# Final RMS norm: applying the scale per token as the transposed rows leave PSUM

## The reference

```python
def rmsnorm(x, g):
    xf = x.astype(jnp.float32)
    y = xf * lax.rsqrt(jnp.mean(xf * xf, axis=-1, keepdims=True) + RMS_EPS)
    return (y * g.astype(jnp.float32)).astype(x.dtype)

def trunk(x, S_init, make_ctx, attend):
    for l in range(DEPTH):
        ...
        x = x + o
        x = x + sq_relu_mlp(rmsnorm(x, norm_mlp[l]), w_mlp_up[l], w_mlp_down[l])
    return rmsnorm(x, norm_final), jnp.stack(new_S), new_kv
```

## Time and profile before

| | us |
|---|---|
| median of 3 runs | 2034.08 (2032.62 to 2037.61) |
| the profiled execution | 2034.55 |
| its span, first to last instruction | 2032.9 |
| TensorE busy (matmul) | 1908.7 (94%) |
| VectorE, ScalarE, GpSimd busy | 896.5 (44%), 489.1 (24%), 417.0 (21%) |

### The profile page before, as it was taken

One profiled execution on the slowest core, in us unless ns is written; L12 is line 12 of the kernel. 1 busy time (PEld: TensorE's weight loads), 2 busy tenths in 40 slices (PEclk: granted clock), 3 DMA queues, 4 the chain that ended last, 5 costly groups with the idle time before them and its releaser, 6 DMA issues.

```text
span 2032.9 us, 27497 instructions
## 1 busy us (share of the span) xinstructions
PE 1908.7 (94%) x10540; PEld 1588.8 (78%) x10540; DVE 896.5 (44%) x1296; ACT 489.1 (24%) x1007; POOL 417.0 (21%) x613
## 2 busy tenths in 40 slices
PE   6999999898999999999989989799867899999997
PEld 6888888677888888888856668687535788888886
DVE  3555555515453535310157763244520355353544
ACT  3344434321101010200235543233310211111101
POOL 2232433210000000200036653342020100000002
PEclk9999999899999999999979999899988999999998
DMA  5232221112222222223850008896997022222221
GB/s 146 72 87 64 65 75 64 64 42 83 83 83 83 83 83 84 94 72 95 221 126 1 1 1 173 207 190 159 300 303 245 1 83 83 83 83 83 83 83 43
DMA packets 164708, 207.22 MB, mean 102 GB/s; under 512 B 13905, under 2 KB 101570, under 8 KB 164450
## 3 DMA queue, kind: packets, MB, share of 16 engines
q1 hardware_dynamic: 146818, 186.84, 31.9%
q10 hardware_dynamic: 16416, 14.95, 2.3%
q0 software_dynamic: 1344, 3.67, 0.5%
HBM read 194.33 MB, written 18.42 MB: 105 GB/s over the span
## 4 chain that ended last, share of the span: by engine, by line
PE 85%; DVE 3%; ACTq 2%; DMA 2%; SPq 2%; issue 2%; ACT 2%; POOL 1%; DVEq 0%; POOLq 0%
PE ps L1209 39%; PE ps L1000 12%; PE ps L1039 11%; PE ps L1300 5%; PE ps L1293 3%; PE ps L1079 2%; DMA stream<-in_cache_nsa_kv 2%; PE ps L1054 2%; PE ps L1349 1%; ACTq L2007 1%; PE ps L1371 1%; PE ps L1389 1%; ACTq L428 1%; PE ps L1145 1%; PE ps L1105 1%
## 5 line engine op out<-in xcount | busy, mean ns | idle before, releaser
L1039 PE MATMUL ps<-h,stream 128*128 128x260 f32 x1024 | 236.3, 385 | 5.1 <-DVE h L2129 5.1
L1209 PE MATMUL ps<-big,scratch 128*128 128x260 f32 x1024 | 232.3, 382 | 0.0
L1039 PEld LDWEIGHTS ps<-h,stream 128*128 128x128 f32 x1024 | 191.3, 191 | 37.0 <-issue 10.0
L1209 PEld LDWEIGHTS ps<-big,scratch 128*128 128x128 f32 x1024 | 194.6, 190 | 29.9
L2276 DVE TENSOR_TENSOR scratch<-stream 128x1024 f32<-128x1024 f32 x64 | 106.1, 1699 | 223.6 <-PE ps L1209 214.8
L796 POOL TENSOR_TENSOR big<-big 128x520 f32<-128x520 f32 x32 | 51.7, 1616 | 713.5 <-ACT big L1820 713.5
L1209 PE MATMUL ps<-big,stream 128*128 128x260 f32 x768 | 176.2, 382 | 0.0
L1209 PEld LDWEIGHTS ps<-big,stream 128*128 128x128 f32 x768 | 145.9, 190 | 22.4
L1000 PE MATMUL ps<-h,stream 128*128 128x260 f32 x640 | 142.4, 386 | 1.7 <-DVE h L2705 1.7
L1000 PEld LDWEIGHTS ps<-h,stream 128*128 128x128 f32 x640 | 122.7, 192 | 21.1 <-DVE h L2705 1.9
L1209 PE MATMUL ps<-h,stream 128*128 128x260 f32 x512 | 120.2, 389 | 9.1 <-DVE h L2299 9.1
(11 more groups left out here) (363 smaller groups left out, 3016.6 us busy)
## 6 DMA issues: line engine op xcount, KB each, us to landing
stream<-in_w_mlp_up SPq DMA_DIRECT2D x16, 2048.0 KB, 8.1
stream<-in_w_mlp_down SPq DMA_DIRECT2D x16, 2048.0 KB, 7.9
stream<-in_cache_nsa_kv SPq DMA_DIRECT2D x128, 256.0 KB, 6.1
stream<-in_w_hgrn_in SPq DMA_DIRECT2D x32, 512.0 KB, 6.9
stream<-in_cache_nsa_kv SPq DMA_DIRECT2D x114, 128.0 KB
stream<-in_cache_nsa_kv ACTq DMA_DIRECT2D x114, 128.0 KB
stream<-in_cache_win_kv SPq DMA_DIRECT2D x16, 512.0 KB
out<-in_cache_win_kv SPq DMA_DIRECT2D x8, 1022.0 KB
```

The lines of the kernel that those rows point to most:

```text
L1039: m = nc.tensor.matmul(pair(c)[:, a, :], w[:, k, :], h[:, k, NH * a:NH * a + NH], start=(k == 0), stop=(k == KD - 1))
L1209: m = nc.tensor.matmul(ps[:, BANK[r] + q, 0:NH], w[:, k, q, :], operand(p, r)[:, k, :], start=(r not in (2, 3, 4) and k == 0), stop=(k == ...
```

## The change

The norm's gain and its per-token scale are taken apart.

The gain moves to ScalarE, as the first layer does it: `mlp_act(1, GAIN_FINAL)` writes `h = x * gain` as each piece of `x` becomes final. The transposes then turn `h` without the token's scale, so they need not wait for the norm: groups 0 and 1 come ahead of the sum of squares (they use banks 6 and 7), groups 2 and 3 right behind it, 4 to 7 after those.

The sum of squares is made with the roles swapped: the squares are the stationary operand and one column of ones the moving one, so token `i` of a tile comes out on partition `i`. There are five tiles (four of 128 tokens, one of 8), and `rstd` is 128 by 5 in place of 128 by 520. Tiles 0 and 1 need only GpSimd's sum; tiles 2 to 4 also take rows 4 and 6. Tile 2 holds tokens 256 to 259 of the first half, for which rows 4 and 6 are in the sum already, so GpSimd sets those columns to zero first.

The copies out of PSUM become multiplications by the token's scale, a number for each partition: `tensor_scalar` on VectorE, `activation` with a scale on ScalarE.

```diff
+        Y_BANK = (6, 7, 0, 1, 2, 3, 6, 7)
...
-        out_count = {..., "final": 6 * KD + 4}
+        out_count = {..., "final": 6 * KD + 8}
...                                                        # GpSimd, mlp_pool
                 joined(last)
+                if name == "final":
+                    ch.link(nc.gpsimd.memset(squares[:, 4:8:2, 2 * P:NH], 0.0))
                 piece_added(3, 1, 1)
...                                                        # TensorE
-            norm_sum("final", squares)
+            def rows_turned(u):
+                a, cg = u % TT, u // TT
+                if u >= 6:
+                    pe.wait_ge(ydone[u % 2], 1)
+                for c in range(4):
+                    m = nc.tensor.transpose(ps[:, Y_BANK[u], P * c:P * c + P], h[:, 4 * cg + c, P * a:P * a + P], ident[:])
+                m.then_inc(yturned, 1)
+
+            until(pe, "u2", 2 * PAIRS)
+            pe.wait_ge(norm["out"], out_count["mlp1"] + 4)
+            rows_turned(0)
+            rows_turned(1)
+            pe.wait_ge(norm["added"], turn_of["final"])
+            until(pe, "c", 2 * PAIRS)
+            for a in range(TT + 1):
+                cols = slice(P * a, min(P * a + P, N))
+                rows = (0,) if a < 2 else (0, 4, 6)
+                if a == 2:
+                    pe.wait_ge(norm["sq"], steps_before(SQ_STEPS, "final") + 5)
+                for k in rows:
+                    m = nc.tensor.matmul(ps[0:cols.stop - cols.start, 5, a:a + 1], squares[:, k, cols], ones[:, 0:1],
+                                         start=(k == 0), stop=(k == rows[-1]))
+            m.then_inc(norm["sum"], 1)
+            until(pe, "dve_a", kind_count(2 * PAIRS, "down"))
+            rows_turned(2)
+            rows_turned(3)
             until(pe, "d", 2 * PAIRS)
-            until(pe, "dve_a", kind_count(2 * PAIRS, "down"))
-            for u in range(2 * TT):
-                a, cg = u % TT, u // TT
-                if a == 0:
-                    pe.wait_ge(norm["out"], out_count["final"] - KD // 2 * (1 - cg))
-                if u >= 4:
-                    pe.wait_ge(ydone[u % 2], (u - 4) // 2 + 1)
-                for c in range(4):
-                    m = nc.tensor.transpose(ps[:, u % 4, ...], h[:, 4 * cg + c, ...], ident[:])
-                m.then_inc(yturned, 1)
+            pe.wait_ge(norm["out"], out_count["final"])
+            for u in range(4, 2 * TT):
+                rows_turned(u)
+            for p in range(2):
+                pe.wait_ge(ydone[p], 2)
             for c in range(KD):
-                m = nc.tensor.transpose(ps[0:B, 4 + c // 4, ...
+                m = nc.tensor.transpose(ps[0:B, c // 4, ...
...                                                        # ScalarE
-            mlp_act(1)
-            root("final")
+            mlp_act(1, GAIN_FINAL)
+            act.wait_ge(norm["sum"], turn_of["final"] + 1)
+            nc.scalar.activation(rstd[:, 0:TT], ps[:, 5, 0:TT], ACT.Sqrt, bias=eps[:], scale=1.0 / D).then_inc(norm["sqrt"], 1)
+            nc.scalar.activation(rstd[0:B, TT:TT + 1], ps[0:B, 5, TT:TT + 1], ACT.Sqrt, bias=eps[0:B], scale=1.0 / D)\
+                .then_inc(norm["sqrt"], 1)
+            act.wait_ge(token_rstd, 1)
             for u in range(1, 2 * TT, 2):
                 act.wait_ge(yturned, u + 1)
-                nc.scalar.activation(yrows[...], ps[:, u % 4, :], ACT.Copy).then_inc(ydone[1], 1)
+                nc.scalar.activation(yrows[...], ps[:, Y_BANK[u], :], ACT.Copy,
+                                     scale=rstd[:, u % TT:u % TT + 1]).then_inc(ydone[1], 1)
...                                                        # VectorE
-            norm_dve("final")
-            for k in range(KD):
-                nc.vector.scalar_tensor_tensor(out=h[:, k, :], in0=x[:, k, :], scalar=vec[...], in1=rstd[:], ...)
+            n = steps_before(SQRT_STEPS, "final")
+            dve.wait_ge(norm["sqrt"], n + 2)
+            nc.vector.reciprocal(rstd[:, 0:TT], rstd[:, 0:TT]).then_inc(token_rstd, 1)
+            nc.vector.reciprocal(rstd[0:B, TT:TT + 1], rstd[0:B, TT:TT + 1]).then_inc(token_rstd, 1)
+            dve.wait_ge(token_rstd, 2)
             for u in range(0, 2 * TT, 2):
                 dve.wait_ge(yturned, u + 1)
-                nc.vector.tensor_copy(yrows[...], ps[:, u % 4, :]).then_inc(ydone[0], 1)
+                nc.vector.tensor_scalar(yrows[...], ps[:, Y_BANK[u], :], rstd[:, u % TT:u % TT + 1], None, ALU.mult)\
+                    .then_inc(ydone[0], 1)
```

More of the change, by code:

```diff
@@ L269, in steps_before @@
             return sum(steps[other] for other in steps if turn_of[other] < turn_of[name])
-        out_count = {"mix0": KD, "mlp0": 2 * KD, "kv": 3 * KD + 4, "attn": 4 * KD + 4, "mlp1": 5 * KD + 4, "final": 6 * KD + 4}
+        out_count = {"mix0": KD, "mlp0": 2 * KD, "kv": 3 * KD + 4, "attn": 4 * KD + 4, "mlp1": 5 * KD + 4, "final": 6 * KD + 8}
         squares = scratch[:, 0:KD * N].rearrange("p (k t) -> p k t", k=KD)
@@ L381, in hybrid_step @@
         block = ctx.enter_context(nc.Block())
-        hready = sem("hready")
+        hready, token_rstd = sem("hready"), sem("token_rstd")
         ydone, ysdone = [sem("ydone0"), sem("ydone1")], sem("ysdone")
@@ L970, in norm_sum @@
                 n = turn_of[name]
-                if name in ("attn", "final"):
+                if name == "attn":
                     pe.wait_ge(norm["added"], n)
@@ L1636, in _ @@
+            m.then_inc(norm["sum"], 1)
+            until(pe, "dve_a", kind_count(2 * PAIRS, "down"))
+            rows_turned(2)
+            rows_turned(3)
+            until(pe, "d", 2 * PAIRS)
+            pe.wait_ge(norm["out"], out_count["final"])
[3 more added lines that the diff above has]
+                pe.wait_ge(ydone[p], 2)
             for c in range(KD):
-                m = nc.tensor.transpose(ps[0:B, 4 + c // 4, P * (c % 4):P * (c % 4) + P], h[:, c, T:N], ident[:])
+                m = nc.tensor.transpose(ps[0:B, c // 4, P * (c % 4):P * (c % 4) + P], h[:, c, T:N], ident[:])
@@ L2084, in _ @@
             norm_act("mlp1", squares, added("nsa_out"), early=[(GAIN_MLP + KD, gained_h)])
-            mlp_act(1)
-            root("final")
+            mlp_act(1, GAIN_FINAL)
[4 more added lines that the diff above has]
+            act.wait_ge(token_rstd, 1)
             for u in range(1, 2 * TT, 2):
                 act.wait_ge(yturned, u + 1)
-                nc.scalar.activation(yrows[:, u % TT, 512 * (u // TT):512 * (u // TT) + 512], ps[:, u % 4, :], ACT.Copy)\
-                    .then_inc(ydone[1], 1)
+                nc.scalar.activation(yrows[:, u % TT, 512 * (u // TT):512 * (u // TT) + 512], ps[:, Y_BANK[u], :], ACT.Copy,
+                                     scale=rstd[:, u % TT:u % TT + 1]).then_inc(ydone[1], 1)
         @block.vector
@@ L2710, in _ @@
             mlp_pairs(1)
-            norm_dve("final")
-            for k in range(KD):
-                nc.vector.scalar_tensor_tensor(out=h[:, k, :], in0=x[:, k, :],
-                                               scalar=vec[:, GAIN_FINAL + k:GAIN_FINAL + k + 1], in1=rstd[:],
-                                               op0=ALU.mult, op1=ALU.mult).then_inc(norm["out"], 1)
+            n = steps_before(SQRT_STEPS, "final")
[3 more added lines that the diff above has]
+            dve.wait_ge(token_rstd, 2)
             for u in range(0, 2 * TT, 2):
                 dve.wait_ge(yturned, u + 1)
-                nc.vector.tensor_copy(yrows[:, u % TT, 512 * (u // TT):512 * (u // TT) + 512], ps[:, u % 4, :])\
-                    .then_inc(ydone[0], 1)
+                nc.vector.tensor_scalar(yrows[:, u % TT, 512 * (u // TT):512 * (u // TT) + 512], ps[:, Y_BANK[u], :],
+                                        rstd[:, u % TT:u % TT + 1], None, ALU.mult).then_inc(ydone[0], 1)
             dve.wait_ge(yturned, 2 * TT + 1)
-            nc.vector.tensor_copy(ysrows.rearrange("p (c n) -> p c n", c=2), ps[0:B, 4:6, :]).then_inc(ysdone, 1)
+            nc.vector.tensor_scalar(ysrows.rearrange("p (c n) -> p c n", c=2), ps[0:B, 0:2, :], rstd[0:B, TT:TT + 1], None,
+                                    ALU.mult).then_inc(ysdone, 1)
 _INS = ["x_prompt", "x_sample", "cache_nsa_kv", "cache_win_kv", "state_hgrn", "page_table", "norm_mix", "norm_mlp",
```

1 line of the change is left out of this document (removed).

## The result

| | before | changed |
|---|---|---|
| median of 14 runs, us | 2036.82 (2032.03 to 2040.82) | 2028.32 (2023.76 to 2031.97) |
| ratio to before, 95% interval | | 0.9956 (0.9947 to 0.9966) |
| profiled execution: own time, span | 2034.55, 2032.9 | 2023.76, 2022.1 |

The changed kernel is faster by 8.5 us, 0.44%.

The account below looks back on a forecast made before the run. The end was taken to stand 7.74 us behind the first store's issue; replacing 11.46 us from sum to issue by 2.12, less 0.80 for the dearer sum, saves 8.54: from median 2034.08 to 2025.5, range 2023.3 to 2028.3.

Parts of the forecast that it names:

- gain rows, memset: ScalarE's gain rows beside the last pair's products and GpSimd's 0.10 us memset of a few columns: costed at nothing.
- transposes ahead and two sums done: Eight transposes (0.8 us) and two sums (0.43) in TensorE's hole before the last square ends, done at about 2012.2.
- sum of squares ends: Nine one-column matmuls behind the last square end at 2014.50, 0.80 us later than before (bounds 0.5 to 1.0).
- first store issued: SyncE's first 1 MB store, set by the copies of groups 0 to 3, moves from 2025.16 to 2016.62.
- tail shortened by: First store's issue falls 8.54 us earlier and the end follows, to 2024.36.
- The central step: The stores, not the transposes, set the end, which stands 7.74 us behind the first issue.
- Root, reciprocal and hand-overs: Between sum and copies, two narrow roots and two reciprocals with hand-overs: 0.7 us taken, bounds 0.5 to 1.2.
- the copies: VectorE copies groups 0 and 2 in 1.28 us; ScalarE takes 0.60 plain or 0.72 scaled each; these set the first store.
- The step on the clock: TensorE keeps full clock in the new tail, since 0.50 showed only behind a 7 us idle stretch; transposes take 0.10 us.
- Rival 1: Clock falls to 0.50 from the first wait at about 2012; 5.4 us gained, 2028.7; chance 0.08.
- Rival 2: Stores run slower beside busy copying engines and TensorE, 300 GB/s: 1.5 us lost, 2027.0; chance 0.10.
- Rival 3: TensorE runs out of instructions in the tail; a stall decides from 8.5 us up, 13.3 gives 2038.8; chance 0.03.

Follow-up runs that it names:

- e5: Kernel before with the gain alone moved to ScalarE, wide root and reciprocal kept, VectorE multiplying eight rows by the scale; tail 20.90 us (21.05 before).
- e3: Changed kernel with the first 1 MB store held back until all eight groups are copied, so both go together; tail 15.00 us (12.33 in the changed kernel).
- e10: Kernel of e2 with nine useless transposes filling TensorE's pause between the sum and the scale; tail 16.74 us.
- e2: Changed kernel with all groups turned only when the per-token scale is ready; tail 15.23 us, first store at 7.42.
- e11: Kernel of e2 run once more, unchanged; tail 14.87 us, first store at 7.04.
- e4: Kernel before with 64 useless transposes in TensorE's idle stretch between the sum and the first rows; tail 20.50 us (21.05 before).
- e1: Changed kernel with groups 0 and 1 turned right behind the sum of squares instead of ahead of it; tail 12.88 us (12.33 in the changed kernel).
- e7: Kernel of e6 with the two 1 MB stores cut into four of 512 KB, each issued when its pair is copied; tail 11.34 us, ratio to before 0.9960.
- e6: Changed kernel with row 0's sum matmuls of all five tiles and group 1's transposes ahead of the last square, sums in another bank; tail 11.95 us.
- e8: Kernel of e7 with the sums' bank cleared by its first matmul alone and group 1 turned behind the sum; tail 11.22 us, ratio to before 0.9953.
- e9: Kernel of e3 run once more, unchanged; tail 13.72 us, first issue at 5.98.

## Why the prediction was right

Its steps, measured from the last square's start (2011.85 in the prediction's times):

| step | predicted | measured |
|---|---|---|
| gain rows, memset | hidden | hidden: 21.02 us for the last pair (again in e5: 21.01) |
| transposes ahead and two sums done | 0.35 | 0.52, still ahead of the square's end |
| sum of squares ends | 2.65 | 2.42 |
| VectorE's first scaled copy | 3.38 | 3.13 |
| first store issued | 4.77 | 4.57 |
| from there to the end | 7.74 | 7.76 |
| tail shortened by | 8.54 | 8.72 |

The central step, that the end follows the first store and not the transposes, was confirmed in each of the 14 profiled executions: the end stood 7.74 to 7.84 us behind the first issue, with that issue anywhere from 3.4 to 13.3 us behind the square. The spread of 0.1 is that of the printed span.

The term that was mis-sized is the sum of squares. The prediction has 1.28 us for the six matmuls with full weights, 0.54 for the three with 8-column weights and 0.14 for the last one's end. The stretches of the changed kernel show the six and then the three (columns as in the earlier trace rows):

```profile
2010.46:2011.88 1.42, 1.42 (x12) 1.41 (x12) 0.00 (x0) 0.76 (x2) 0.00 (x0) 1.00 0.04 12
2011.88:2012.12 0.24, 0.24 (x8) 0.20 (x7) 0.00 (x0) 0.00 (x0) 0.00 (x0) 1.00 0.00 0
```

The six took 1.42 us (0.24 each, not 0.21) and the three 0.24 (0.08 each, not 0.18), and 0.07 passed to the sum's end. Two errors of opposite sign, 0.14 too little and 0.30 too much, partly cancelled; what was left is the 0.2 us by which all later steps came early. Where it did no harm: the two sums ahead waited for x21, which was added only 0.1 us before the square began, and so ended at 0.52 and not at 0.35, while the square released the rest at 0.69.

Root, reciprocal and hand-overs (0.73 predicted from the sum's end to VectorE's copy, 0.71 measured) and the copies (1.39 predicted, 1.35 by the rows it names, 1.44 measured to the store) were right to 0.05 us.

The median itself came 2.8 us above the forecast of 2025.5, though the difference was met within 0.1 of a microsecond: the three runs of before from which I started (median 2034.08) lay 2.7 us under the median of fourteen. So 2028.32 stands at the very top of the range, which ended at 2028.3, and that it did not fall clearly outside is luck. A forecast of a time inherits the error of its baseline, and the range should carry it.

The step on the clock came true, but its reason does not hold. I held that the clock falls only behind a long gap. e3 lost it in the changed kernel's own sequence, where TensorE's weight loads had paused for no more than 0.22 us since the products, and e10 lost it during the sum, 1.8 us behind the square, after a pause of 0.9 us ahead of it. So a clock of 1.00 in the changed kernel's profiles is in part luck: of the four executions with its TensorE program one lost it. Rival 1 describes something that occurs here. The Trainium skill's "TensorE: Matmul & The Clock Gate" (section "A second HAM failure mode: psum-queue depth-cycling") has the clock swing when TensorE pauses briefly and often between groups, as it cycles through PSUM banks; e3's fall came behind two short pauses (0.22 and 0.17 us), but no run shows that they were its cause. Rival 1's price was wrong for the place where the fall was seen: it came at 3.7 us, when groups 0 to 3 had been turned, not at the first wait. Where it strikes before they are turned, as in e2 and e11, it costs 1.4 and 1.1 us by the estimate above. Rival 2 (slower stores) did not occur: 376 GB/s. Rival 3 did not either: the longest wait of a weight load in the tail is 0.22 us.

What the gain consists of can be followed by the first store's issue, step by step. Before it stood at 13.31 us behind the square. With the clock kept it stands at 12.72 (e4). With the narrow root and reciprocal, the gain moved and the scaling in the copies, but every row still turned behind the scale, it would stand at about 6.0 at full clock (the estimate under e2); 0.25 of that step is the gain's move alone (e5). With the rows turned from the sum on it stands at 5.12 (e1), and with two groups ahead of the sum at 4.57. So some 6.7 of the 8.7 us come from the narrow root and reciprocal and the scaling in the copies, 1.4 from turning the rows earlier and 0.6 from the clock. Without the estimate, e2 as it ran, with the clock lost as in the kernel before, has 5.9 of them (13.31 to 7.42). The root and reciprocal and the scaled copies were never separated from each other.

## What to carry to other kernels

When a kernel ends in stores that fill the DMA engines, find the issue of the first one and ask what it waits for: the end moved with it one for one in all 14 executions here, as long as the later stores came early enough to leave no hole, and cutting the first store smaller cost nothing that could be seen (e7). A per-token factor was cheap here where tokens lie on partitions, 128 by 5 numbers in place of 128 by 520 (0.18 us for the reciprocal in place of 3.40), and it can be applied by the copy that leaves PSUM anyway. When the long part ahead varies by more than the change is worth, measure the tail of the profile from an event that both kernels share, and keep the baseline's error in the range.

## What the runs showed of the hardware

- Several sums in one PSUM bank, each started by its own matmul before the others were finished, came out wrong. In e6 and e7 the prompt rows of `y` are off by some 3,300 times their size, while the sample rows, whose tile was started last, are right; with one start for the whole bank (e8) both are right. The reading that fits is that a start flag resets more of a bank than the column that its matmul writes, so that the later second parts replaced the first part of tiles 2 and 3 instead of adding to it: where the second part is zero (tokens 256 to 259) only the small constant is left under the root. No run looked at the sums themselves, and e8 also turns group 1 later, so this is argued and not shown.
- The same TensorE instructions met a granted clock of 1.00 in e9 and of 0.50 from 3.7 us on in e3; with a filler of 64 transposes over 7.1 us it stayed at 1.00 in e4, where it had fallen to 0.50 in the same place before and in e5.
- A reciprocal of 128 by 4 took 0.18 us, of 128 by 520 3.40; two independent small ones start 0.09 us apart.
- A scaled copy of 128 by 512 out of PSUM took 0.69 us on ScalarE and 0.75 on VectorE when alone, against 0.60 and 0.69 unscaled; four back to back on VectorE took 2.73 us.
- A float32 matmul with one moving column took 0.24 us of TensorE with full weights and 0.08 with 8-column weights; the transposes of a 128 by 128 block came 0.11 us apart at a granted clock of 1.00 and 0.21 at 0.50.
